# A one-layer hybrid decoder step: attention with two sets of score banks, the samples' products spread over the stage and into the output projection, and beta and decay columns in strips

## The reference

```
proj = x @ w_in                       # ..., q|k|v (1536), beta (4), decay (4), gates
beta = sigmoid(beta_raw);  logdecay = -exp(a_log) * softplus(dec_raw + dt_bias)
...                                   # two branches, merged; h = LN(alpha*x + mixed @ w_o)
xq = (h @ w_xq).reshape(B, L, 4, 256)
sc = einsum('blhd,bmhd->bhlm', xq, mem_k) * 256 ** -0.5
pr = softmax(sc)                      # over 256 memory tokens
xo = einsum('bhlm,bmhd->blhd', pr, mem_v).reshape(B, L, 1024) @ w_xo
h  = LN(alpha*h + xo);  y = LN(alpha*h + relu(h @ w_ff1)^2 @ w_ff2)
```

## Time and profile before

| | |
|---|---|
| Time, median of 3 runs | 1174.79 us (1170.83 to 1175.11) |
| The profiled execution, its own time | 1174.75 us |
| its span in the trace | 1173.0 us |
| PE busy | 1131.3 us (96%) |
| DVE / ACT / POOL busy | 526.8 / 429.8 / 412.9 us |
| granted PE clock, mean | 0.989 of full speed |

### The profile page before, as it was taken

One profiled execution on the slowest core, in us unless ns is written; L12 is line 12 of the kernel. 1 busy time (PEld: TensorE's weight loads), 2 busy tenths in 40 slices (PEclk: granted clock), 3 DMA queues, 4 the chain that ended last, 5 costly groups with the idle time before them and its releaser, 6 DMA issues.

```text
span 1173.0 us, 23013 instructions
## 1 busy us (share of the span) xinstructions
PE 1131.3 (96%) x9685; PEld 1079.8 (92%) x9685; DVE 526.8 (45%) x959; ACT 429.8 (37%) x769; POOL 412.9 (35%) x209
## 2 busy tenths in 40 slices
PE   7999999999999999999898999999999989999996
PEld 6998879898999999998897689999999989999995
DVE  4789648773675535866102336532122112112237
ACT  5456205132143522337434334762133123213314
POOL 4343141011132434455541153555343333433302
PEclk9999989999999999999999999999999999999998
DMA  7224414001127233324655552223223222222102
GB/s 228 89 74 154 114 54 133 22 20 37 37 91 83 91 90 94 104 90 126 234 178 197 205 191 57 88 88 111 91 73 91 81 65 90 77 86 76 51 1 82
DMA packets 41613, 115.62 MB, mean 99 GB/s; under 512 B 14385, under 2 KB 16945, under 8 KB 39089
## 3 DMA queue, kind: packets, MB, share of 16 engines
q1 hardware_dynamic: 35632, 109.09, 29.3%
q10 hardware_dynamic: 5888, 5.18, 2.2%
HBM read 103.26 MB, written 7.53 MB: 94 GB/s over the span
## 4 chain that ended last, share of the span: by engine, by line
PE 59%; issue 26%; POOL 9%; DMA 4%; DVE 2%; ACT 0%; SPq 0%; POOLq 0%; ACTq 0%; DVEq 0%
PE bank L567 53%; POOL w_lo L509 9%; DMA kv<-v 2%; PE bank L1047 1%; DMA kv<-kT 1%; PE bank L621 1%; PE bank L992 1%; PE bank L749 0%; PE bank L598 0%; DMA xraw<-xT 0%; DVE qkv L1676 0%; PE bank L726 0%; PE bank L631 0%; PE bank L1009 0%; SPq L473 0%
## 5 line engine op out<-in xcount | busy, mean ns | idle before, releaser
L509 POOL TENSOR_TENSOR w_lo<-w_raw,w_hi 128x1024 fp32r<-128x1024 f32 x84 | 208.6, 2485 | 385.0 <-ACT w_hi L1144 385.0
L567 PE MATMUL bank<-x_hi,w_hi 128*128 128x288 f32 x640 | 195.2, 305 | 9.0 <-DVE x_lo L1646 8.5
L567 PE MATMUL bank<-x_lo,w_hi 128*128 128x288 f32 x640 | 190.0, 297 | 0.0
L567 PE MATMUL bank<-x_hi,w_lo 128*128 128x288 f32 x640 | 189.4, 296 | 0.0
L1144 ACT ACTIVATE w_hi<-w_raw 128x1024 fp32r<-128x1024 f32 x116 | 122.9, 1060 | 165.5 <-PE bank L567 117.5
L567 PEld LDWEIGHTS bank<-x_hi,w_hi 128*128 128x128 f32 x640 | 121.2, 189 | 15.0 <-POOL w_lo L509 8.4
L567 PEld LDWEIGHTS bank<-x_hi,w_lo 128*128 128x128 f32 x640 | 121.6, 190 | 0.0
L567 PEld LDWEIGHTS bank<-x_lo,w_hi 128*128 128x128 f32 x640 | 121.5, 190 | 0.0
L547 POOL TENSOR_TENSOR w_lo<-w_raw,w_hi 128x1024 fp32r<-128x1024 f32 x28 | 67.4, 2407 | 106.2 <-ACT w_hi L1144 106.2
L547 POOL TENSOR_TENSOR w_lo_more<-w_raw,w_hi_more 128x1024 fp32r<-128x1024 f32 x28 | 67.1, 2396 | 101.0 <-ACT w_hi_more L1144 101.0
L567 PE MATMUL bank<-hid_hi,w_hi 128*128 128x288 f32 (+2 forms) x256 | 76.5, 299 | 0.0
(11 more groups left out here) (412 smaller groups left out, 3124.1 us busy)
## 6 DMA issues: line engine op xcount, KB each, us to landing
w_raw<-w SPq DMA_DIRECT2D x152, 512.0 KB, 3.5
kv<-kT SPq DMA_DIRECT2D x8, 1024.0 KB, 8.1
kv<-v SPq DMA_DIRECT2D x8, 1024.0 KB, 8.8
u<-u SPq DMA_DIRECT2D x32, 105.5 KB, 2.4
xraw<-xT SPq DMA_DIRECT2D x4, 576.0 KB, 6.0
sst<-sdelta SPq DMA_DIRECT2D x4, 512.0 KB, 5.2
sdelta_out<-sst ACTq DMA_DIRECT2D x4, 512.0 KB, 3.9
yT<-res SPq DMA_DIRECT2D x8, 192.0 KB, 2.0
```

The lines of the kernel that those rows point to most:

```text
L509: nc.gpsimd.tensor_tensor(wlo[:, s], raw[:, s % RAW], whi[:, s].bitcast(f32), sub)\
L567: ins = nc.tensor.matmul(bank[:, 0:b - a], lhsT=w[:, kb], rhs=cols_of(m, kb, a, b), start=(opens and i == 0 and j == 0), stop=(closes and ...
```

## The change

Two parts of the kernel change.

**Beta and decay.** `wbd` is allocated 32 columns wide, of which SP loads 8 and POOL clears 24. `beta_decay` becomes 16 plain fp32 matmuls from the unsplit `x` (`xraw`), 32 output rows each: input block kb goes to strip kb % 4, so that four strips each hold a part of the sum over the width. ACT copies all 128 rows; the five transposes become five matmuls with `fold`, which adds the strips and turns the result. `fold` is made early, by DVE, ahead of the first taps of the short convolution and after a wait for `cst_loaded`. The split of the columns on ACT and DVE is gone.

**Attention.** Odd heads use banks 4 and 5, even ones 0 and 1, for scores and for the transposes after them; `ap`, `amax`, `asum` exist twice. The order of PE, ACT and DVE is written anew. `own_product` is cut into `own_first` and `own_second` (two heads each). The wait for `taken[1]` stands behind `scores(0)`. The last product of the samples, `own_product(1, 1)`, moves into the output projection, behind its third chunk, with banks 6 and 7, and its `flip_samples` behind the fourth; ACT's and DVE's parts of it move into the work on the blocks. ACT's wait for the stores moves ahead of `sample_exps(0)`, because the second `ap` lies over `pst`.

```
-    wbd = at("wbd", 46.5, [P, KB, 8])
-    bdw = pair("bdw", 46.75, KB, 8)
+    wbd = at("wbd", 44.5, [P, KB, 32])
...
-        sp.dma_start(wbd[:], A["wbd"][:]).then_inc(S("par_loaded"), 16)
+        sp.dma_start(wbd[:, :, 0:8], A["wbd"][:]).then_inc(S("par_loaded"), 16)
...
-            pe.wait_ge(S("bdw_split"), 2)
+            pe.wait_ge(S("par_loaded"), 48)
+            pe.wait_ge(S("bd_zero"), 1)
             for kb in range(KB):
+                g = kb % 4
                 for h, half in enumerate(HALVES):
-                    for j, (w, m) in enumerate(((bdw[0], x[0]), (bdw[0], x[1]), (bdw[1], x[0]))):
-                        ins = nc.tensor.matmul(ps[4 + h][0:8, 0:HALF], lhsT=w[:, kb], rhs=m[:, kb, half],
-                                               start=(kb == 0 and j == 0), stop=(kb == KB - 1 and j == 2))
+                    ins = nc.tensor.matmul(ps[4 + h][32 * g:32 * g + 32, 0:HALF], lhsT=wbd[:, kb], rhs=xraw[:, kb, half],
+                                           start=(kb < 4), stop=(kb >= 4))
...
-            ins = T.transpose(ps[6][0:n, 8 * t:8 * t + 8], bdr[:, t * P:t * P + n], ident[0:8, 0:8])
+            ins = T.matmul(ps[6][0:n, 8 * t:8 * t + 8], lhsT=bdr[:, t * P:t * P + n], rhs=fold[:, 0:8], start=True, stop=True)
...
         pe.wait_ge(taken[0], O_XO // 2)
-        pe.wait_ge(taken[1], O_XO // 2)
+
+        def score_bank(h, i):
+
+            return ps[4 * (h % 2) + i]
 
         def scores(h):
-
-            if h:
-                pe.wait_ge(S("att_exp"), 4 * h)
+            if h >= 2:
+                pe.wait_ge(S("att_pt"), 2 * (h - 1))
...
         scores(0)
-        own_product(0, 0)
+        pe.wait_ge(taken[1], O_XO // 2)
+        own_first(0, 0, ps[2])
+        own_second(0, 0, ps[3])
+        scores(1)
         flip(0)
-        scores(1)
+        flip_samples(0, 0, ps[2])
         values(0)
-        flip_samples(0, 0)
         flip(1)
-        own_product(0, 1)
         scores(2)
+        own_first(0, 1, ps[2])
+        own_second(0, 1, ps[3])
         values(1)
-        flip_samples(0, 1)
         flip(2)
         scores(3)
-        own_product(1, 0)
         values(2)
+        flip_samples(0, 1, ps[3])
+        own_first(1, 0, ps[2])
         flip(3)
+        own_second(1, 0, ps[3])
         values(3)
-        flip_samples(1, 0)
-        own_product(1, 1)
-
-        pe.wait_ge(S("ao_lo"), KB)
-        pe.wait_ge(S("att_exp"), TILES * X_HEADS)
+        flip_samples(1, 0, ps[2])
+
         for p, part in enumerate(HALVES):
             for n in range(KB):
                 k = p * KB + n
                 if p == 0:
                     pe.wait_ge(lo_ready, C_XO + n + 1)
-                if k == RING - 1:
+                if k == KB:
                     pe.wait_ge(S("sao_lo"), GROUPS)
                 if k >= RING:
                     pe.wait_ge(S("half_taken"), k - RING + 1)
-                half_gemm(k, n, part, ao, every)
-                if k == 1:
-                    flip_samples(1, 1)
+                if k == 2:
+                    pe.wait_ge(S("s_pt"), GROUPS)
+                half_gemm(k, n, part, ao, [(kb, (S("ao_lo"), kb + 1)) for kb in range(KB)] if k == 0 else every)
+                if k == 2:
+                    own_first(1, 1, ps[6])
+                    own_second(1, 1, ps[7])
+                if k == 3:
+                    flip_samples(1, 1, ps[7])
...
-        act.wait_ge(stored, 16 * (4 + 2 * CT))
+        block_square(0, 0)
+        act.wait_ge(S("kv_used"), 16)
+        split(C_XO + 4)
+        split(C_XO + 5)
+        samples_hi(1, ps[7])
         split(C_XO + 6)
         split(C_XO + 7)
-        for j in range(KB):
+        for j in range(1, KB):
             block_square(0, j)
...
-        dve.wait_ge(S("bdw_split"), 1)
-        V.tensor_tensor(bdw[1][:], wbd[:], bdw[0][:].bitcast(f32), sub).then_inc(S("bdw_split"), 1)
...
+        dve.wait_ge(S("cst_loaded"), 16 * (3 + CT))
+        V.tensor_reduce(fold[:], ident.rearrange("p (t c) -> p c t", c=32), X, add).then_inc(S("fold_ready"), 1)
...
         dve.wait_ge(S("att_pt"), 2 * X_HEADS)
-        for j in range(KB):
+        block(0, 0)
+        block(0, 1)
+        sample_outputs(1, 6)
+        samples_lo(1, ps[7])
+        for j in range(2, KB):
             block(0, j)
```

More of the change, by code:

```diff
@@ L490, in _ @@
             nc.gpsimd.memset(ones[:, i], v).then_inc(S("consts"), 1)
+        nc.gpsimd.memset(wbd[:, :, 8:32], 0.0).then_inc(S("bd_zero"), 1)
         nc.gpsimd.memset(eps_ln, LN_EPS).then_inc(S("consts"), 1)
@@ L1031, in values, with own_heads @@
             ins.then_inc(S("att_o"), 1)
[L1033 to L1042, removed]
+        def own_heads(g, part, pair, bank):
+            for h in (2 * pair, 2 * pair + 1):
                 for d in range(2):
@@ L1046, in own_product, with own_first, own_second, flip_samples @@
                     for i in range(4):
-                        ins = T.matmul(ps[2 + h // 2][32 * i:32 * i + 32, h % 2 * 256:(h % 2 + 1) * 256], lhsT=mine,
+                        ins = T.matmul(bank[32 * i:32 * i + 32, h % 2 * 256:(h % 2 + 1) * 256], lhsT=mine,
                                        rhs=kv[:, i, a:a + 256], start=(d == 0), stop=(d == 1))
-            ins.then_inc(S("kv_used"), 4)
-        def flip_samples(g, part):
+            return ins
+        def own_first(g, part, bank):
+            if part:
+                pe.wait_ge(S("s_pt"), g + 1)
+            for i in range(4):
+                pe.wait_ge(S(f"kv_loaded{i}"), 16 * (2 * g + part + 1))
+            own_heads(g, part, 0, bank)
+        def own_second(g, part, bank):
+            if g and not part:
+                pe.wait_ge(S("sao_lo"), g)
+            own_heads(g, part, 1, bank).then_inc(S("kv_used"), 4)
+        def flip_samples(g, part, bank):
             pe.wait_ge(*((S("sout"), 2 * (g + 1)) if part else (S("s_exp"), X_HEADS * (g + 1))))
             for kb in range(KB):
-                ins = T.matmul(tiled(ps[2 + part][:, kb * GT:(kb + 1) * GT], DEC_SEQ),
+                ins = T.matmul(tiled(bank[:, kb * GT:(kb + 1) * GT], DEC_SEQ),
                                lhsT=aps[:, kb // 2, kb % 2 * P:(kb % 2 + 1) * P], rhs=own_rows, start=True, stop=True)
@@ L1230, in _ @@
         for h, half in enumerate(HALVES):
-            A_(bdr[:, half], ps[4 + h][0:8, 0:HALF], ACT.Copy).then_inc(S("bd_rows"), 1)
+            A_(bdr[:, half], ps[4 + h][:, 0:HALF], ACT.Copy).then_inc(S("bd_rows"), 1)
         q_sigmoid(QT - 1)
@@ L1469, in exps @@
             act.wait_ge(S("att_max"), 3 * (h + 1))
[L1470 to L1471 removed]
+            if h >= 2:
+                act.wait_ge(S("att_flip"), h - 1)
             for t in range(TILES):
[L1473 to L1474 removed]
+                A_(ap[h % 2][:, t], ps[4 * (h % 2) + t // 2][:, (t % 2) * N_MEM:(t % 2 + 1) * N_MEM], ACT.Exp,
+                   bias=amax[h % 2][:, t:t + 1], accum_out=asum[h % 2][:, t:t + 1]).then_inc(S("att_exp"), 1)
         def flipped(h):
@@ L1480, in flipped @@
             for mb in range(2):
-                A_(apt[:, mb], ps[4 + mb][:, :], ACT.Copy).then_inc(S("att_pt"), 1)
+                A_(apt[:, mb], ps[4 * (h % 2) + mb][:, :], ACT.Copy).then_inc(S("att_pt"), 1)
         def out_hi(h):
@@ L1494, in sample_exps, with samples_hi @@
                    accum_out=sasum[:, h:h + 1]).then_inc(S("s_exp"), 1)
-        def samples_hi(g):
+        def samples_hi(g, bank):
             act.wait_ge(S("s_flip"), 2 * g + 2)
-            A_(ao[0][:, :, SEQ + g * GT:SEQ + (g + 1) * GT], tiled(ps[3][:, 0:KB * GT], GT), ACT.Copy)\
+            A_(ao[0][:, :, SEQ + g * GT:SEQ + (g + 1) * GT], tiled(bank[:, 0:KB * GT], GT), ACT.Copy)\
                 .then_inc(S("sao_hi"), 1)
         exps(0)
+        act.wait_ge(stored, 16 * (4 + 2 * CT))
         sample_exps(0)
@@ L1512, in _ @@
         out_hi(2)
+        samples_hi(0, ps[3])
         flipped(3)
@@ L1713, in stationary @@
                 dve.wait_ge(S("u4_loaded"), 16 * 16)
-                own.step(V.tensor_reduce(fold[:], ident.rearrange("p (t c) -> p c t", c=32), X, add))
+                dve.wait_ge(S("fold_ready"), 1)
                 own(V.memset(w4[96:128].rearrange("p g (j k) -> p g j k", k=CONV_K)[:, :, :, CONV_K - 3], 0.0))
@@ L2153, in maxima @@
         def maxima(h):
+            top = amax[h % 2]
             dve.wait_ge(S("att_sc"), h + 1)
[L2156 to L2159, removed]
+            for i in range(2):
+                row_max(top[:, 2 * i:2 * i + 2], ps[4 * (h % 2) + i])
             dve.wait_ge(S("att_max"), 3 * h + 2)
-            V.tensor_scalar(amax, amax, -1.0, None, mul).then_inc(S("att_max"), 1)
+            V.tensor_scalar(top, top, -1.0, None, mul).then_inc(S("att_max"), 1)
         def probs(h):
+            total, mine = asum[h % 2], ap[h % 2]
             dve.wait_ge(S("att_exp"), TILES * (h + 1))
-            ch(V.reciprocal(asum, asum))
-            V.tensor_tensor(ap[:], ap[:], bc(asum, N_MEM), mul).then_inc(S("att_p"), 1)
+            ch(V.reciprocal(total, total))
```

(13 more changed lines are left out.)

28 lines of the change are left out of this document (11 added, 17 removed).

## The result

The changed kernel takes 1152.49 us, median of 4 runs (1151.36 to 1154.18); the kernel before took 1173.78 us beside it, median of 4. The ratio is 0.9828, 95% interval [0.9807, 0.9849]: 21.3 us less, where 12.75 were predicted. That the kernel is faster was right, how much was wrong.

The account below looks back on a forecast made before the run. PE, busy 96% of the span, was taken as the bound, so only less matmul time or closed gaps help. 9.0 + 4.05 - 0.3 = 12.75 us off 1174.75 gave 1162.0 us, range 1158.5 to 1168.0.

Parts of the forecast that it names:

- the line of the sum for beta and decay: q, k and v stage: 48 matmuls (6.32 us) become 16 (2.25 us), gain 4.05, less 0.3 for the turning matmuls.
- The attention term: Attention stage: the new order closes PE's waits for transfers and at the start; gain 9.2 us, taken as 9.0.
- Rival B: Beta and decay: strips wait for program order, 4.5 us, gain 1.8 instead of 4.05, time 1164.3; chance 0.12.
- The turning matmuls: Five transposes become fp32 matmuls, 1.1 us instead of 0.37; 0.3 of the 0.7 more counted, bounds 0 and 0.7.
- ACT's and DVE's split: Column split for beta and decay, dropped: nobody on PE waited for it beyond 0.2 us.
- Product to product: Attention: distances between successive products of the samples, some 18.4, 17.3 and 19.4 us, the last with 9.5 us of projection.
- At the keys: Attention, group 1: PE finishes its other work 0.3 us before the keys land.
- The wait for `taken[1]`: Start of attention: placed behind scores(0), it covers PE's 1.00 us wait for ACT's last copy of the queries.
- Rival C: Clock: low-level stretches of 3.5 us in attention's sparse work, or small waits, give 1164 to 1167; chance 0.13.
- D: Attention: the last transfer is not overlapped by the projection; gain 0.8 instead of 9.0, time 1170.2; chance 0.10.
- E: Slower: PE stays at 1.2 GHz through the denser mixture; decides from some 19 us of low-clock work; chance 0.05.

Follow-up runs that it names:

- the second trace of before: The kernel before, unchanged, run and profiled again: 1170.91 us, ratio 0.9997.
- The padded kernels: The kernel before with 16 tiny fp32 matmuls put ahead of PE's q, k and v products, run twice: 1165.56 us (0.9940) and 1167.08 us (0.9938).
- att_pad16: The kernel before with only the attention part, plus 16 tiny matmuls ahead of the q, k and v products: 1157.77 us, ratio 0.9873.
- after_pad10: The changed kernel with 10 tiny matmuls ahead of the q, k and v products: 1159.31 us, ratio 0.9907.
- after_pool_later: The changed kernel with POOL's adds for `h1w` waiting for the samples' last maxima: 1152.27 us, ratio 0.9833.
- same_after: The changed kernel, unchanged, run and profiled again: 1153.27 us, ratio 0.9844.
- after_again: The changed kernel, unchanged, run once more beside the padded kernels and the beta part alone: 1154.55 us, ratio 0.9829.
- attention_only: The kernel before with only the attention part of the change: 1163.23 us, ratio 0.9929.
- after: The changed kernel with both parts, first run, against the kernel before: 1152.49 us, ratio 0.9828.

## Why the prediction was wrong

**The step that failed** is the line of the sum for beta and decay, 4.05 less 0.3. It priced the removed instructions only at their own place. What it left out is that they, and all behind them, are also PE's program: with them gone the loop of the MLP is no longer fetched again, 5.4 us in the profiled pair (89.24 to 83.87), 4.5 against the second trace of before (88.38). The padded kernels, at 6.9 and 7.2 by their times, confirm the direction and the place, and not that size. The issue row at 945 and the half clock behind it were in the trace of before. The prediction works out attention and the q, k and v stage, and puts the MLP at nothing without a reason.

**A second step failed the other way.** The attention term, 9.0, was too large: 6.17 us in the profiled pair, 6.2 and 6.6 by times beside the new beta, 8.6 on the kernel before. The missing term and what changed outside both parts, 10.35 us in the pair, hid that.

**Beta and decay at their own place.** 4.17 gained in the chunks with `beta_decay`, against 4.05. The strips run beside each other: 16 matmuls in 2.12 us, though neighbours share a strip. Rival B (one round for each pair, 4.5 us) is refuted. The Trainium skill's rule in "TensorE: Matmul & The Clock Gate", Part 3, that matmuls start and end in the order of the program, which the prediction put beside B, disagrees with the 2.12 us as far as matmuls to different strips go. The turning matmuls cost 0.74 where 0.3 were taken and 0.7 was the bound: DVE's slack did not hide them. That nobody on PE waited more than 0.2 us for ACT's and DVE's split was mis-sized: before, ACT waits 2.7 us for DVE until it copies the first results (L1172, at 22.72), after, it copies at 20.08. PE's first two chunks are 0.65 us shorter in the pair, and 0.6 to 1.8 over the eight traces with the new beta.

**Attention.** The mechanism was right in each step, and the size was not. Product to product takes 18.37, 17.38 and 22.72 us; 18.4, 17.3 and 19.4 were forecast. The third has the 1.19 us behind L2197, 0.2 in `flip_samples`, and 1.6 in the first three chunks (11.11 instead of 9.5), of which a part ran at the half clock. At the keys PE waits 0.6 us, where 0.3 were worked out. So scores(0) to the fifth chunk took 70.50 us where the sum gives 75.47 - 8.0 = 67.5. Three traces of the new order (att_pad16, after_pad10, after_pool_later) have 67.58 to 67.66, two more (same_after, after_again) 68.96 and 68.93, and attention_only, with 6.8 us at the half clock, 72.11. The sum gives the new order at its best. The old one is not as constant as one trace made it look either: 71.65 to 75.47 us over six. The prediction subtracted from a trace at the upper end, with a low-clock stretch in it. The means are 74.0 over the six and 69.0 over the seven, 5.0 us apart where 8.0 were forecast. The wait for `taken[1]` gave 1.20 against 1.00. Why the times give 8.6 us on the kernel before and 6.2 to 6.6 beside the new beta stays open.

**The clock.** Rival C feared new stretches at the half level. The changed kernel's trace has one in attention, 3.4 us at 666, as the kernel before has at 646, and two are gone, 6.8 us at 157.9 and 3.4 at 949.8. Four of four traces with the wait for issue have a stretch right behind it, none of the other ten. Five of the six with the old attention have one in attention, two of the seven with the new order as changed. Where it follows a wait of PE, closing the wait gives back its length and half of the stretch behind it. The one at 155 to 160 comes and goes in kernels of either kind (none in after and same_after, 3.4 us in after_again); the 2.58 us gained there in the profiled pair are no gain of the change.

**D and E.** The last transfer is met by the projection, and no long stretch at the half clock came.

**Open.** The first memory products are 1.3 us shorter after (7.25 to 7.30 with the new beta, 7.78 with its padding; 7.87 to 8.67 in the kernel before, its repeat, its padded versions and attention alone), but also 7.19 in the padded attention part, so it is not a matter of the beta part alone. In the profiled pair PE waits at these products for POOL's low parts, 2.4 us before and 1.1 after; why they come earlier was not followed. Nor was it tried to turn the loop into straight code, or to place the loop on purpose; at which places it is fetched again is known for eight programs of PE, not as a rule.

## What to carry to other kernels

Read every "issue" row in the chain of an engine that is otherwise never idle: at the branch back of a long loop it can be code that is fetched again, and it moves with any edit ahead of the loop, so one that adds or removes instructions can gain or lose time where it changes nothing, here 4.5 to 7.5 us of the MLP's stretch. Before a gain is put down to an edit, pad both kernels and look at the number of packets in the instruction queue, and go through the padded traces stretch by stretch, since padding moved other things too (4.9 us at the start here). Subtract from a stretch of several traces, not of one, where the old code waits for transfers.

The fastest seen are the changed kernel and the one with POOL's later start, 1152.3 to 1154.6 us, not to be told apart.

## What the hardware showed that was not expected

The second turn of the loop costs 2.7 to 3.2 us at the branch (in after_pad10 2.1 more five matmuls later) and a stretch of 3.4 or 6.8 us at 1.2 GHz behind it, and 9 packets of 16 KB more, by the place of the code alone. Sixteen plain fp32 matmuls of 288 columns in four strips take 2.12 us although neighbours share a strip. A DVE operation on 128 x 4 elements took 0.17 us with POOL idle and up to 1.44 us while POOL added [128 x 576] tiles, ending 0.02 to 0.03 us after the end of one add in twelve traces. The Trainium skill, "SBUF — State Buffer", under "Who interferes with whom", names `tensor_scalar`, which this one is, among the DVE operations that can enter a mode in which DVE and GpSimd block each other for a whole instruction, and `tensor_reduce` as one that never does on this chip; the traces agree, with the reductions at 1.29 us either way.
